# Attention of two layers rebuilt as one staggered stage each, sink heads first, and the scan's convolution done in place

## The chip, the cores and the metric

One core of a Trainium2 chip runs the whole program. The metric is device microseconds of that core, the median of several runs. TensorE (PE; its weight loads are PEld in the profile), VectorE (DVE) and ScalarE (ACT) compute. The weights come through SyncE's DMA queue. GpSimd does nothing.

## The reference, cut to what matters

Two blocks of two layers each act on 256 latent and 256 context tokens of width 1024, everything in float32. Block one has a gated linear attention layer and a state-space layer (SSD), whose scan starts with a depthwise convolution of width 5 and a SiLU. Block two has an even and an odd attention layer, and the odd one ends in a mixture of experts. Of the two attention layers the reference computes:

```python
# even: 8 heads of width 64, rms norm on q and k; latent queries see 256 latent keys with a position bias,
# masked by column, and 256 context keys; context queries see the context keys alone
s_loc = einsum(q, k) * 64**-0.5 + where(col_ok, rpb[...], -1e30)
p = softmax([s_loc, q @ k_ctx.T * 64**-0.5]);  out = p @ [v, v_ctx]
# odd: 8 "c" heads (2 key heads, window of 128, a sink in the denominator), 4 "d" heads, q and k with rms norm and rope
p_c = softmax([window scores, context scores], extra=sink)
p_d = softmax(q1 @ k1.T) - lam * softmax(q2 @ k2.T);  out_d = rms_norm(p_d @ v) * subln_g * (1 - LAM_INIT)
# SSD
xbc = silu(dwconv(xbc, conv_w, conv_b))
```

## The kernel before

Activations are kept transposed (features on partitions, tokens along the free axis). `run` walks a list of stages. Each stage has three streams of instructions, one for TensorE, one for ScalarE and one for VectorE, written out by hand. Within a stage the engines meet only at semaphores. Between two stages stands a barrier (each engine drains and waits for the other two), unless the stage is `joined`. TensorE's products go round six PSUM banks in the order of the stage. `Banks.empty` makes TensorE wait until a bank has been read, `Banks.full` makes a reader wait for its product, and `release` drains and frees. Weights are 2 MB blocks in four slots, which SyncE fills again when `W.used` says that a block is finished.

Even layer, stage by stage: `EvenProject` (24 product tiles: gate b, c, u, then q, k, v; L1587), `BiasLoad` (L1637: ScalarE issues 16 DMAs for the position bias, and TensorE flips the landed rows in six products), `HeadNorm` (L1666: for each of eight head tiles Square on ScalarE, a block-ones product on TensorE, Ln and Exp on ScalarE, a scaling on VectorE), and `Attention` with 32 items of 128 queries (L1719). An item is: score product(s) "s", 0.125 and bias on VectorE into SBUF, maximum and its negative there (L1796 to L1803), exponential with its sum on ScalarE (L1770), reciprocal and normalising on VectorE (L1818, L1822), four or two transposes "t" on TensorE (L1746), a copy on ScalarE (L1780), output products "o" with v as the stationary operand (L1753), and a copy on VectorE (L1809). The scores of item n+1 are issued ahead of the transposes of item n.

Odd layer: `OddProject` (21 tiles, L1926), `HeadNorm` over 13 head tiles with a second pass of 13 rotation products (L1685) for rope, `KeysAndLambda` (L1979: both key heads are doubled over the partitions, and lambda), `Attention` with 16 window items that have a sink, a barrier, `Attention` with 8 differential items of two score maps each (L1825, L1826 combine them), and `SubNorm` (L2009).

The scan, `SsdGroups` (L1312): eight groups of eight steps. While group g steps, group g+1 is projected, convolved on VectorE (L1473, L1475: five taps from `s_raw` into one of two accumulators `s_acc`), put through SiLU on ScalarE (L1440: from `s_acc` into its place, one tile behind each convolution), and transposed. The steps themselves need Exp on ScalarE (L1455, L1459) for steps 4 to 7 of a group. SiLU and Exp are in different table sets of ScalarE.

Of the kernel before, what the change touches and what calls it, by code (L numbers as in the profile page):

```python
# [15 lines left out]
ALU = mybir.AluOpType  # L16
# [3 lines left out]
P = 128  # L20
# [156 lines left out]
def build(nc, I, out, stop=None):  # L177
    ctx = ExitStack()
    with ctx:
# [37 lines left out]
        for n in ("loads", "setup_rows", "sil", "mod_lat", "mod_ready", "centred", "squares", "rstd_used", "root", "normed",  # L217
# [4 lines left out]
                  "free_a", "free_b", "free_c", "free_d", "bias_loads", "rope_in", "convd", "ada_rows", "ada_cols", "ada_copied", "ada_free", "moe_loads", "da_done", "ready", "lam", "picked", "placed", "gate_cols", "overflow_known", "moe_rl", "guest_rows", "guest_copied", "guest_cols", "guest_read"):  # L222
# [1004 lines left out]
        s_acc = arena_at(11168, 2, TOK)  # L1227
# [84 lines left out]
        class SsdGroups(Stage):  # L1312
# [5 lines left out]
            def __init__(self):  # L1318
                N, order = 8 * NG, []

                def ahead(g, n):
# [104 lines left out]
            def act(self, act, B, ch):  # L1426
                for ev in self.order:
# [9 lines left out]
                    if kind == "convolve":  # L1437
                        T = LAT if j == 3 else TOK
                        act.wait_ge(*S("convd").taken("act"))
                        act.activation(self.feat(k, j)[:, 0:T], s_acc[:, j % 2, 0:T], ACT.Silu,  # L1440
                                       bias=vc("conv_b", self.tile(k, j))).then_inc(*S("feat").given())
# [20 lines left out]
            def dve(self, dve, B, ch):  # L1462
                for ev in self.order:
                    kind, k, j = ev
                    i = self.index.get(ev)
                    if kind == "convolve":
# [17 lines left out]
                    if kind == "overlap":  # L1484
                        dve.wait_ge(*S("feat").taken("dve", 2))
# [90 lines left out]
        m_q = arena_at(4096, 8, TOK)  # L1576
# [3 lines left out]
        m_bias = arena_at(13824, 8, 6, GRID)  # L1580
        m_pad = arena_at(15872, 4, 2 * (LAT + 2))
        m_gc = arena_at(6144, 4, TOK)
        m_s = [[uT[:, 2 * i + j, :] for j in range(2)] for i in range(2)]
        m_pt = [uT[:, 4 + i, :] for i in range(2)]
        sinks = sb("sinks", [P, 8])

        class EvenProject(Stage):  # L1587
            products = 24
            joined = True

            def pe(self, pe, B):
                w_in = I["ev_w_in_2"][0]
                for c in range(6):
                    w = W.block(pe, [w_in[:, c * 512:c * 512 + 512]], KD)
                    if c == 0:
                        first_features(pe, B, [(j, w, j * P, P) for j in range(4)], TOK)
                    for j in range(4 if c else 0):
                        if c == 5:
                            token_major(pe, B, 4 * c + j, w, 0, 512, uT, KD, j)
                        else:  # L1600
                            feature_major(pe, B, 4 * c + j, w, j * P, uT, KD, 0, TOK)
                    W.used(full_sem, B.base + 4 * c + 4)

            def act(self, act, B, ch):
                for i in range(8):
                    bank = B.full(act, i)
                    act.activation((m_g if i < 4 else m_gc)[:, i % 4, :], bank[:, :], ACT.Copy).then_inc(*B.free(i))
                for i in range(12, 24, 2):
                    bank = B.full(act, i)
                    act.activation(self.dst(i), bank[:, :], ACT.Copy).then_inc(*B.free(i))  # L1610

            def dst(self, i):
                return [m_q, m_k, m_v][(i - 12) // 4][:, i % 4, 0:512]

            def dve(self, dve, B, ch):
                dve_link(ch, dve.memset(arena[:, 15872:15872 + 8 * (LAT + 2)], 0.0))
                for j in range(4):
# [16 lines left out]

        m_braw = arena_at(16896, 8, 6, GRID)

        class BiasLoad(Stage):  # L1637

# [800 lines left out]
```

## Time and profile before

| | |
|---|---|
| median of three runs | 3602.71 us (3601.45 to 3604.27) |
| time of the profiled execution, its span | 3605.16 us, 3603.4 us |
| TensorE busy, mean granted clock | 3213.0 us (89%), 0.92 |
| VectorE, ScalarE busy | 1328.3 us (37%), 557.3 us (15%) |

| stretch, us from the span's start | what runs |
|---|---|
| 1043 to 1465 | `SsdGroups` |
| 1788 to 1955 | `EvenProject` |
| 1955 to 1999 | `BiasLoad`, `HeadNorm` |
| 1999 to 2140 | `Attention`, even |
| 2683 to 2783 | `OddProject` |
| 2783 to 2828 | `HeadNorm`, `KeysAndLambda` |
| 2828 to 2927 | `Attention`, window items |
| 2927 to 2990 | `Attention`, differential items |
| 2990 to 2997 | `SubNorm` |

A float32 product shows as two MATMUL records, a transpose as one. The granted clock is 1.00 at 2.4 GHz and 0.50 at 1.2 GHz; a value between is a mean over a stretch.

### The profile page before, as it was taken

How to read it: one execution, taken by the hardware profiler on the slowest of the kernel's cores; microseconds unless marked ns; L12 is line 12 of the kernel's file. 1: busy time of each engine (PE TensorE's matmuls, PEld its weight loads, DVE VectorE, ACT ScalarE, POOL GpSimd, SP SyncE). 2: the span in 40 equal slices, each digit the busy share in tenths (PEclk: the TensorE clock that was granted, in tenths of full speed). 3: DMA queues.
4: the chain of work that ended last, by engine and by line, in shares of the span. 5: the costliest groups of instructions: out<-in, count | busy, mean ns of one | idle time of the engine just before them, and what ended most of it. 6: DMA issues, size and time to landing. Idle time of an engine off the chain costs nothing.

```text
span 3603.4 us, 31613 instructions
## 1 busy us (share of the span) xinstructions
PE 3213.0 (89%) x12574; PEld 2029.4 (56%) x12574; DVE 1328.3 (37%) x3165; ACT 557.3 (15%) x1077; POOL 0.2 (0%) x4
## 2 busy tenths in 40 slices
PE   7996889999987877899997779999999666999999
PEld 2446344444565555688743344444455335799998
DVE  2655365477426566411210433533010553001011
ACT  1111110000214334120100321000011222100000
POOL 0000000000000000000000000000000000000000
PEclk9998889999988988899998779999999657999999
DMA  7530145565241111145313002543322002478885
GB/s 247 181 128 1 46 152 187 152 188 189 70 117 47 38 33 47 61 151 150 117 70 87 1 1 94 187 136 105 96 85 91 0 0 71 169 252 289 278 269 204
DMA packets 382833, 431.46 MB, mean 120 GB/s; under 512 B 15257, under 2 KB 291384, under 8 KB 382554
## 3 DMA queue, kind: packets, MB, share of 16 engines
q1 hardware_dynamic: 281840, 329.77, 27.9%
q10 hardware_dynamic: 100842, 99.62, 8.6%
q8 instruction: 102, 1.67, 0.2%
q14 instruction: 49, 0.40, 0.0%
HBM read 428.32 MB, written 1.05 MB: 119 GB/s over the span
## 4 chain that ended last, share of the span: by engine, by line
PE 80%; DVE 11%; ACT 3%; issue 3%; DVEq 1%; DMA 1%; ACTq 0%
PE bank L813 48%; PE bank L2178 9%; PE bank L830 5%; PE bank L2192 4%; PE bank L838 4%; PE bank L1753 2%; PE bank L517 2%; PE bank L1746 1%; DVE arena L1475 1%; DVE small L1800 1%; PE bank L2160 1%; DVE uT L1798 1%; ACT L1455 1%; PE bank L2204 1%; DVE arena L1505 1%
## 5 line engine op out<-in xcount | busy, mean ns | idle before, releaser
L813 PE MATMUL bank<-uT,slot 128*128 128x512 f32 (+2 forms) x2848 | 1071.6, 535 | 2.1 <-DVEq L2364 2.1
L813 PEld LDWEIGHTS bank<-uT,slot 128*128 128x128 f32 (+1 forms) x2848 | 539.2, 191 | 480.9 <-issue 455.4
L813 PE MATMUL bank<-arena,slot 128*128 128x512 f32 (+1 forms) x2016 | 695.7, 507 | 30.6 <-DVEq L2364 30.6
L813 PEld LDWEIGHTS bank<-arena,slot 128*128 128x128 f32 x2016 | 387.7, 194 | 318.8 <-issue 279.0
L560 DVE SCALAR_TENSOR_TENSOR arena<-arena,sT 128x256 f32<-128x256 f32 x784 | 333.7, 481 | 8.0
L2178 PE MATMUL bank<-arena,slot 128*128 128x128 f32 x2816 | 317.6, 276 | 5.1 <-issue 4.4
L2178 PEld LDWEIGHTS bank<-arena,slot 128*128 128x128 f32 x2816 | 316.7, 193 | 7.9 <-issue 7.8
L886 DVE SCALAR_TENSOR_TENSOR hT<-bank,mod,hT 128x256 f32<-128x256 f32 (+1 forms) x104 | 41.6, 439 | 419.2 <-PE bank L813 419.2
L830 PE MATMUL bank<-uT,slot 128*128 128x512 f32 (+1 forms) x448 | 168.5, 541 | 24.4 <-ACT uT L582 12.5
L2263 DVE TENSOR_TENSOR arena<-bank,halves 128x256 f32<-128x256 f32 (+1 forms) x48 | 19.3, 403 | 435.6 <-ACT halves L2224 435.6
L2192 PE MATMUL bank<-slot,arena 128*128 128x256 f32 x704 | 153.3, 379 | 1.0 <-DVEq L144 1.0
L830 PEld LDWEIGHTS bank<-uT,slot 128*128 128x128 f32 x448 | 92.7, 209 | 99.8 <-issue 92.8
L2192 PEld LDWEIGHTS bank<-slot,arena 128*128 128x128 f32 x704 | 133.7, 190 | 19.3 <-issue 1.2
L838 PE MATMUL bank<-slot,uT 128*128 128x512 f32 (+3 forms) x416 | 133.5, 478 | 5.7 <-issue 5.7
L1746 PE MATMUL bank<-const,uT 128*128 128x128 f32 x192 | 50.3, 403 | 94.2 <-DVE uT L1822 63.0
L669 ACT ACTIVATE halves<-hT 128x512 f32<-128x512 f32 (+1 forms) x49 | 26.4, 540 | 576.6 <-DVE hT L886 576.6
L1746 PEld LDWEIGHTS bank<-const,uT 128*128 128x128 f32 x192 | 30.7, 198 | 148.3 <-DVE uT L1822 108.9
L953 DVE TENSOR_TENSOR arena<-halves 128x512 f32<-128x512 f32 (+1 forms) x64 | 35.8, 559 | 202.3 <-ACT halves L943 202.1
L838 PEld LDWEIGHTS bank<-slot,uT 128*128 128x128 f32 x416 | 69.6, 201 | 68.3 <-issue 68.2
L560 DVE SCALAR_TENSOR_TENSOR rstd<-arena,sT,rstd 128x256 f32<-128x256 f32 x224 | 90.0, 480 | 0.0
L1475 DVE SCALAR_TENSOR_TENSOR arena<-arena,vectors 128x512 f32<-128x512 f32 (+1 forms) x128 | 87.7, 685 | 4.6
L517 PEld LDWEIGHTS bank<-const,arena 128*128 128x128 f32 x448 | 61.6, 195 | 41.5 <-issue 27.0
(295 smaller groups left out, 2458.1 us busy)
## 6 DMA issues: line engine op xcount, KB each, us to landing
arena<-in_ada_w ACTq DMA_DIRECT2D x88, 1024.0 KB, 5.2
slot<-in_ffn_w SPq DMA_DIRECT2D x42, 2048.0 KB, 8.9
slot<-in_moe_w SPq DMA_DIRECT2D x32, 2048.0 KB, 10.4
slot<-in_moe_w SPq DMA_DIRECT2D x32, 1408.0 KB, 8.8
slot<-in_moe_w SPq DMA_DIRECT2D x16, 1536.0 KB, 9.2
slot<-in_gla_w_in SPq DMA_DIRECT2D x6, 2048.0 KB, 10.3
slot<-in_ev_w_in SPq DMA_DIRECT2D x6, 2048.0 KB, 8.0
slot<-in_ffn_w SPq DMA_DIRECT2D x8, 1408.0 KB, 6.8
```

Source lines behind the costliest of these rows:

```text
L517: ins = pe.matmul(ada_cols_bank[:, o:o + 1], acc[:, s, j * P:j * P + P], one[:, 0:1], start=True, stop=True)
L560: ins = dve.scalar_tensor_tensor(out=acc[:, s, :], in0=w[:, k, :], scalar=c, in1=acc[:, s, :], op0=ALU.mult, op1=ALU.add)
L813: ins = pe.matmul(bank[0:m, 0:t1 - t0], w[:, k, c0:c0 + m], x[:, k, t0:t1], start=(k == 0), stop=(k == kt - 1))
L830: ins = pe.matmul(bank[0:m, 0:T], w[:, k, c0:c0 + m], uT[:, k, 0:T], start=(k == 0), stop=(k == KD - 1))
L838: ins = pe.matmul(bank[:, 0:c1 - c0], x[:, k, t * P:t * P + P], w[:, k, c0:c1], start=(k == 0), stop=(k == kt - 1))
L886: return dve.scalar_tensor_tensor(out=h, in0=y, scalar=self.m[:, 8 * self.q + k, s:s + 1], in1=h, op0=ALU.mult, op1=ALU.add)
L1455: act.activation(s_cx[k % 2], bank[:, :].rearrange("p (h t) -> p h t", h=4), ACT.Exp).then_inc(*S("ecx").given())
L1475: ins = dve.scalar_tensor_tensor(out=acc, in0=s_raw[:, j, 0:n, tap:tap + LAT], scalar=vc("conv_w", 32 * tap + f), in1=acc, op0=ALU.mult, o ...
L1746: ins = pe.transpose(bank[:, t * P:t * P + P], m_s[n % 2][0][:, t * P:t * P + P], ident)
L1753: ins = pe.matmul(bank[r0:r0 + m, 0:P], v, m_pt[n % 2][:, t * P:t * P + P], start=(t == 0), stop=(t == len(it["v"]) - 1))
L2178: ins = pe.matmul(bank[:, o:o + P], w[:, k, (f - c) * P:(f - c) * P + P], m_x[:, k, e * P:e * P + P], start=(k == 0), stop=(k == KD - 1))
L2192: ins = pe.matmul(bank[:, 0:256], hid[:, k, :], w[:, k, :], start=(k == 0), stop=(k == NFE - 1))
```

## The change

`HeadNorm`, `BiasLoad`, `KeysAndLambda` and `SubNorm` are gone as stages. Their instructions are placed inside the projections and the attention:

- `EvenProject` now runs in the order q, k, b, c, u, v. ScalarE issues the 16 bias DMAs at its start. Eight sums of squares stand between the k and b tiles, seven flips (the bias lies in three pieces) between the c tiles. The bias is kept times 8.
- `OddProject` has 13 sums, 13 rotations ("turn"), the two key doublings ("twin") and lambda between its tiles. VectorE alone takes the q and k tiles out of PSUM; ScalarE takes v.
- There is one `Attention` stage in each layer. The bias is added on TensorE, by a product of the identity and the bias ahead of the latent scores. VectorE takes the maximum from PSUM, and ScalarE's exponential reads PSUM with scale 0.125. Rows are not normalised ahead of the transposes; the output is scaled instead, query by query. In the output product the transposed probabilities are stationary and v moves (64 columns a head, 128 in a differential one), so outputs come with tokens on partitions and are turned back by transposes "f" (four after every 8 even items, two after every 4 window or 2 differential items).
- In the even layer scores run two items ahead, in the odd layer one. The 16 window items come first and the 8 differential ones directly behind them. The norm of a differential output is Square with its sum, Ln and Exp on ScalarE.
- In the scan the convolution accumulates in the tile's final place, and all four SiLUs of a group come behind its last convolution.

```diff
@@ SsdGroups
+                    if n == 4:
+                        out += [("silu", g, j) for j in range(4)]
...
-                        if j >= 2:
-                            dve.wait_ge(*S("feat").taken("dve"))
-                        acc = s_acc[:, j % 2, 0:n * LAT].rearrange("p (s t) -> p s t", s=n)
+                        acc = self.feat(k, j)[:, 0:n * LAT].rearrange("p (s t) -> p s t", s=n)
@@ EvenProject
+                order = [("q", j) for j in range(4)]
+                for j in range(4):
+                    order += [("k", j), ("sum", j)]
+                for j in range(4):
+                    order += [("b", j), ("sum", 4 + j)]
+                for j in range(4):
+                    order += [("c", j), ("flip", 2 * j), ("flip", 2 * j + 1)]
+                order += [("u", j) for j in range(4)] + [("v", j) for j in range(4)]
...
+        def head_sum(pe, B, i, n, T):
+            pe.wait_ge(*S("squares").taken("pe"))
+            bank = B.empty(pe, i)
+            pe.matmul(bank[:, 0:T], half, rl[n % 2][:, 0:T], start=True, stop=True).then_inc(full_sem, 1)
@@ Attention
+                for n in range(-ahead, N + 2):
+                    if n + ahead < N:
+                        order += [("s", n + ahead, j) for j in range(len(items[n + ahead]["maps"]))]
+                    if 0 <= n < N:
+                        order += [("t", n, 0)]
+                    if 0 <= n - 1 < N:
+                        order += [("o", n - 1, 0)]
+                    if n - 2 in turns:
+                        order += [("f", n - 2, 0)]
...
+                            pe.matmul(bank[:, 0:LAT], ident, it["bias"], start=True, stop=False)
+                            pe.matmul(bank[:, 0:LAT], q, k[:, 0:LAT], start=False, stop=True)
+                            pe.matmul(bank[:, LAT:nk], q, k[:, LAT:nk], start=True, stop=True).then_inc(full_sem, 1)
...
-                            ins = pe.matmul(bank[r0:r0 + m, 0:P], v, m_pt[n % 2][:, t * P:t * P + P], start=(t == 0),
+                            ins = pe.matmul(bank[:, 0:w], m_pt[n % 2][:, t * P:t * P + P], v, start=(t == 0),
...
# ScalarE, one turn of the loop over n
+                        act.activation(m_pt[n % 2][:, 0:nk], bank[:, 0:nk], ACT.Copy).then_inc(*B.free(i))
+                            if it["sink"] is not None:
+                                act.activation(es, sinks[:, it["sink"]:it["sink"] + 1], ACT.Exp, bias=nm)
+                            act.activation(s, B[i][:, 0:it["nk"]], ACT.Exp, scale=0.125, bias=nm,
+                                           accum_out=den).then_inc(*B.free(i))
+                            act.drain().then_inc(*S("pr").given())
+                    if 0 <= n - 1 < N and self.items[n - 1]["sub"]:
+                        act.activation(m_turned[:, 0:P], bank[:, 0:P], ACT.Square, accum_out=ssq)
+                        ch.wait(ch(act.drain()))
+                        ch.wait(ch(act.activation(f, ssq, ACT.Ln, scale=1.0 / P, bias=eps)))
+                        act.activation(f, f, ACT.Exp, scale=-0.5).then_inc(*S("root").given())
# VectorE
+                            dve_link(ch, dve.tensor_reduce(mx, bank[:, 0:it["nk"]], AX.X, ALU.max))
...
+                            dve.scalar_tensor_tensor(out=eps, in0=den, scalar=RMS_EPS, in1=den, op0=ALU.mult, op1=ALU.mult)
+                            dve_link(ch, dve.reciprocal(rc1, den1))
+                            dve_link(ch, dve.tensor_scalar(rc, den, rc1, lam_t, ALU.mult, ALU.mult))
+                            dve.scalar_tensor_tensor(out=s0, in0=s1, scalar=rc, in1=s0, op0=ALU.mult,
+                                                     op1=ALU.add).then_inc(*S("pn").given())
...
+                        dve.tensor_scalar(it["o"], bank[:, 0:w], rc, None, ALU.mult).then_inc(*B.free(i))
@@ stages
-        stages += [EvenProject(), BiasLoad(),
-                   HeadNorm(...), Attention(even_items()),
+        stages += [EvenProject(), Attention(*even_attention(), 2),
...
-        stages += [OddProject(), HeadNorm(...), KeysAndLambda(), Attention(window_items()), Attention(diff_items(), lam_t), SubNorm(),
+        stages += [OddProject(), Attention(*odd_attention(), 1),
```

## Rows read from the trace of the kernel before

**Rows 1.** The page: shares of the chain that ended last, TensorE's granted clock in slices.
```profile
PE 80%; DVE 11%; ACT 3%; issue 3%; DVEq 1%; DMA 1%; ACTq 0%
...
PEclk9998889999988988899998779999999657999999
```
**Rows 2.** Busy time by stretches: length, PE, PEld, DVE, ACT, POOL, clock, DMA.
```profile
1203.60:1230.10 26.50, 16.30 (x112) 13.11 (x111) 21.88 (x52) 13.36 (x20) 0.00 (x0) 0.74 0.27 80
...
1788.20:1954.60 166.40, 166.36 (x384) 73.45 (x384) 25.42 (x40) 12.58 (x21) 0.00 (x0) 0.99 0.18 63
1954.60:1998.70 44.10, 16.81 (x29) 5.63 (x28) 10.86 (x15) 14.12 (x24) 0.00 (x0) 0.77 0.36 83
1982.50:1998.70 16.20, 8.71 (x16) 2.46 (x16) 6.01 (x8) 14.00 (x24) 0.00 (x0) 1.00 0.00 0
1998.70:2139.70 141.00, 101.52 (x353) 58.39 (x353) 64.94 (x208) 38.41 (x96) 0.00 (x0) 0.66 0.00 1
...
2683.40:2783.40 100.00, 99.44 (x336) 60.61 (x336) 11.87 (x24) 9.18 (x18) 0.00 (x0) 0.97 0.20 69
2783.40:2828.20 44.80, 24.77 (x58) 10.81 (x58) 25.93 (x58) 17.91 (x41) 0.00 (x0) 0.78 0.14 47
2828.20:2926.60 98.40, 73.76 (x225) 42.88 (x225) 43.43 (x144) 25.58 (x64) 0.00 (x0) 0.55 0.00 1
2926.60:2990.30 63.70, 32.50 (x128) 21.63 (x128) 37.49 (x88) 17.84 (x40) 0.00 (x0) 0.67 0.00 0
2990.30:2996.75 6.45, 1.97 (x9) 1.47 (x9) 2.38 (x6) 4.68 (x12) 0.00 (x0) 0.94 0.00 1
```
**Rows 3.** ScalarE in the scan: table loads, by line and form.
```profile
L1440 ACT ACT_TABLE_LOAD x21 | 26.9, 1283 | 0.4
L1455 ACT ACT_TABLE_LOAD x21 | 26.9, 1283 | 0.4
```
**Rows 4.** The scan, 1092 to 1465: one wait of TensorE; ScalarE in order of time.
```profile
PE bank L1406 <- ACT arena L1451: 41.6, 15, 5.0
...
1209.10 0.72 ACT L1440 ACTIVATE arena<-arena,vectors 128x512 f32<-128x512 f32 x1 [3.44 <-DVE arena L1475]
```
**Rows 5.** Even attention, TensorE in order of time, at the lower clock level.
```profile
2010.54 2.07 PE L1741 MATMUL bank<-arena 64*128 64x512 f32 x2
2013.16 1.97 PE L1753 MATMUL bank<-uT,arena 128*64 128x128 f32 x8
...
2022.02 1.12 PE L1746 MATMUL bank<-const,uT 128*128 128x128 f32 x4 [1.50 <-DVE uT L1822]
2023.07 1.12 PE L1753 MATMUL bank<-uT,arena 128*64 128x128 f32 x4
```
**Rows 6.** The same at the upper level.
```profile
2049.18 1.09 PE L1753 MATMUL bank<-uT,arena 128*64 128x128 f32 x8
2050.20 1.12 PE L1741 MATMUL bank<-arena 64*128 64x512 f32 x2
...
2053.14 0.65 PE L1753 MATMUL bank<-uT,arena 128*64 128x128 f32 x4
2053.72 1.09 PE L1741 MATMUL bank<-arena 64*128 64x256 f32 x2
```
**Rows 7.** Rotation products of the odd `HeadNorm`, six without a wait between them.
```profile
2800.83 2.75 PE L1685 MATMUL bank<-arena,const 128*128 128x256 f32 x12
```
**Rows 8.** Odd attention, 2828 to 2997, by line: ScalarE and VectorE.
```profile
L1770 ACT ACTIVATE uT<-uT,small 128x512 f32<-128x512 f32 x32 | 22.9, 715 | 30.3 <-DVE small L1803 30.3
L1780 ACT ACTIVATE uT<-bank 128x512 f32<-128x512 f32 x24 | 14.3, 598 | 35.2 <-PE bank L1746 35.2
L1770 ACT ACTIVATION_READ_ACCUMULATOR uT<-uT,small 128x1 f32 x32 | 6.0, 188 | 0.0
...
L1800 DVE TENSOR_REDUCE small<-uT 128x1 f32<-128x512 f32 x32 | 22.0, 686 | 4.4
L1826 DVE SCALAR_TENSOR_TENSOR uT<-uT,small 128x512 f32<-128x512 f32 x8 | 6.0, 752 | 0.3
```

More of the change, by code:

```diff
@@ L7 @@
 from contextlib import ExitStack
+import itertools
 import math
@@ L1604, in act @@
[L1604 to L1613, printed above, removed]
@@ new lines, in act @@
+                for n in range(2):
+                    head_square(act, self.head(n)[0], n, TOK)
+                for i, (kind, j) in enumerate(self.order):
+                    if kind == "sum":
+                        rstd_act(act, B, ch, j, i, TOK, 64, RMS_EPS)
+                        if j + 2 < 8:
+                            head_square(act, self.head(j + 2)[0], j + 2, TOK)
+                    if kind in "bc":
+                        bank = B.full(act, i)
+                        act.activation((m_g if kind == "b" else m_gc)[:, j, :], bank[:, :], ACT.Copy).then_inc(*B.free(i))
+                    if kind == "v" and j % 2:
+                        bank = B.full(act, i)
+                        act.activation(m_v[:, j, 0:512], bank[:, :], ACT.Copy).then_inc(*B.free(i))
@@ new lines, in build, with __init__ @@
+        LAM_INIT = 0.8 - 0.6 * math.exp(-0.3)
+        lam_t = small[:, 60:61]
+        sub_gain = small[:, 61:62]
+        class Attention(Stage):
+            def __init__(self, items, turns, ahead):
+                self.items, self.turns, self.ahead = items, turns, ahead
+                self.maps = list(itertools.accumulate(len(it["maps"]) for it in items))
+                N, order = len(items), []
+                for n in range(-ahead, N + 2):
[7 more added lines that the diff above has]
+                        order += [("f", n - 2, 0)]
@@ L1732, in __init__, with score, stats @@
                 self.order = {key: i for i, key in enumerate(order)}
                 self.products = len(order)
+            def score(self, n, j):
+                return m_s[n % 2][j][:, 0:self.items[n]["nk"]]
+            def stats(self, n, j):
+                o = 12 * (n % 4) + 6 * j
+                return [small[:, o + x:o + x + 1] for x in range(6)]
             def pe(self, pe, B):
@@ L1748, in pe @@
                     else:
[L1749 removed]
+                        dst, src, gain, made = self.turns[n]
+                        for m in made:
+                            B.freed(pe, self.order["o", m, 0])
                         bank = B.empty(pe, i)
[L1751 to L1754 removed]
+                        for t, x in enumerate(src):
+                            ins = pe.transpose(bank[:, t * P:t * P + P], x, ident)
@@ L1776, in act @@
+                for n in range(-self.ahead, N + 1):
+                    if 0 <= n < N:
                         i, nk = self.order["t", n, 0], self.items[n]["nk"]
@@ L1839, in even_items, with even_attention @@
+        def even_attention():
+            rows = m_o.rearrange("p (t c) -> p t c", t=4)
+            items, turns = [], {}
             for h in range(8):
@@ new lines, in head @@
+            def head(self, n):
+                kind, j = self.heads[n]
+                x = {"cq": m_ql[:, j, :], "dq": m_ql[:, 4 + j, :], "ck": m_k[:, 0, :], "dk": m_k[:, 2 + j, :]}[kind]
+                return x, f"od_{kind}_g_2", x.shape[1]
+            def pe(self, pe, B):
+                first = dict(cq=0, dq=512, ck=1024, dk=1280, dv=1792)
+                for kind, j in self.order:
+                    i = self.index.get((kind, j))
+                    if kind in first and j == 0:
+                        c = first[kind]
+                        w = W.block(pe, [I["od_w_in_2"][0][:, c:c + (256 if kind == "ck" else 512)]], KD)
+                    if kind == "cq":
+                        if j == 0:
+                            first_features(pe, B, [(n, w, n * P, P) for n in range(4)], LAT)
+                    elif kind == "dq":
+                        feature_major(pe, B, i, w, j * P, uT, KD, 0, LAT)
+                    elif kind == "ck":
```

589 lines of the change are left out of this document (289 added, 300 removed).

## The prediction

> **What bounds the kernel now.** The chain of waits comes first: TensorE carries 80% of it, VectorE 11%, ScalarE 3% [rows 1]. The slices of granted clock beside it show where TensorE is also slow: it is near full almost everywhere, and sags to 0.5 to 0.7 near 2000 us and near 2900 us [rows 1]. Those are the two attention layers. The busy time by stretches then shows three kinds [rows 2]. In the projections TensorE is busy for 166.36 of 166.40 us and 99.44 of 100.00 us at clock 0.97 to 0.99: nothing can be won there but work. Between projection and attention lie 44.1 us (even) and 44.8 us (odd) with 16.8 and 24.8 us of TensorE work, and 6.45 us follow the differential items. In attention itself no engine is full: 141.0 us with TensorE 101.5 at clock 0.66, 98.4 us with 73.8 at 0.55, 63.7 us with 32.5 at 0.67. There the stage is a round trip over three engines, and the clock, which falls in it, stretches TensorE's share of the trip. In the scan a stretch of 26.5 us in each group has TensorE at 16.3 and VectorE at 21.9 [rows 2], and TensorE waits 41.6 us in all for ScalarE's copy L1451, which stands behind an exponential [rows 4].
>
> **The scan.** ScalarE loads a table 42 times in seven groups, 6 a group at 1.28 us [rows 3], because SiLU tiles and exponentials alternate. With the four SiLUs in one place 2 a group are left: 28 loads go, 36 us of ScalarE. More weighs the order: SiLU waits 3.44 us for VectorE's taps [rows 4], and exponentials of the steps queue behind it. What VectorE can give bounds the gain: 26.5 − 21.9 = 4.6 us of idle time in the stretch, and some 2.0 us ahead of it (one load of 1.28 and one SiLU of 0.72), so 6.6 us a group, 46 us. Against it, four SiLUs (three of 0.72, a shorter one) and two loads now make one block of some 5 us, and the exponential of a later step waits behind it; if that block takes all back, the gain is 0. Following the stretch instruction by instruction I get the later steps 4.1 to 4.6 us earlier, so 4.3 x 7 = 30 us.
>
> A switch costs about 2.66 us with its drain by the Trainium skill ("ScalarE: Activation LUTs", What ACT_TABLE_LOAD costs). The load's row of 1.28 us is what the trace has; by the page the 28 switches would be 75 us of ScalarE instead of 36.
>
> **Even layer up to attention.** The 44.1 us go. Into the projections come eight sums of 512 columns and seven flips of 3072 columns together. A record of 512 columns takes 166.4 / 384 = 0.43 us and a product has two [rows 2]: 14 x 0.87 = 12.1 us, with some start cost 13.5. Their feeders are covered: a head costs ScalarE 14.0 / 8 = 1.75 us and VectorE 0.75 us [rows 2], against 6.9 us of TensorE a tile. The bias DMAs are issued first on ScalarE; issue, landing, flips and norm took 44.1 us together, and the first flip comes after 13 tiles, some 90 us. SyncE's queue keeps its order and block sizes. If the cover fails, a sum waits about 2 us. One barrier of some 1.1 us stays.
>
> **Items at the upper clock.** Starts of neighbouring instructions give the price of a group. Output of four blocks: 1.02 us, of two 0.58, scores of 512 columns 1.02 [rows 6], so 0.59 for 256. Four transposes take 1.05 us at the lower level [rows 5], where four output blocks take about 1.9, so 0.57 at the upper one, and two 0.35. The bias product adds 256 columns, 0.43. The new output product loads 128 columns and streams 64 where it loaded 64 and streamed 128; no row shows that. Bounds: half of the old price, and the old one, since the loads would then set the pace. I take the old one, the nearest row. A latent item is 1.45 + 0.57 + 1.02 = 3.05 us of TensorE, a context item 0.59 + 0.35 + 0.58 = 1.52. Two of each and four turning transposes are 9.7 us a head.
>
> The other engines fit under it. ScalarE: copy 0.60, exponential 0.72 + 0.19 [rows 8], some 1.7 us for a latent item. VectorE: maximum 0.69 [rows 8], four small ones of 0.15 to 0.25, some 1.5. The round trip of a window item, where scores run one ahead, is transposes 0.57, copy 0.60, sink exponential 0.30 less overlap, exponential 0.9, handovers: about 2.5 us, under 3.05. So TensorE waits for nobody after the first items: the wait L1746 on L1822 is gone, and late next is TensorE itself. Even attention: 8 x 9.7 = 78, plus 4 for filling and the last turn, 82 us.
>
> Even layer in sum: 44.1 + 141.0 = 185.1 us become 13.5 + 1.1 + 82 = 97: −88.
>
> **Odd layer.** 29 products join the projections: eight sums of 256 and five of 512 columns, 13 rotations, two doublings, lambda. Six rotations took 2.75 us [rows 7], 0.46 each, so 0.6 with a wait before it; 8 x 0.6 + 5 x 1.0 + 13 x 0.6 + 2.3 = 20 us in the place of 44.8. Where a tile is short (1.8 us in "cv") a slot is still 3.0 us, against some 2.2 on VectorE. Window items: 16 x 3.05 and turns, 50.4 us, plus 2.6 barrier and filling, for 98.4. Differential items: TensorE 2.0 + 0.57 + 1.0 = 3.7 us, but the trip is copy 0.6, two exponentials 1.8, combining 0.75 and three small ones 0.6, transposes 0.6, handovers: 4.7 us. TensorE waits 1 us in each and the clock will alternate; at the lower level an item is about 7. I take 5.6: 8 x 5.6 = 45 for 63.7, and 3 us of tail for 6.45. Sum: 44.8 + 98.4 + 63.7 + 6.5 = 213.4 us become 20 + 53 + 45 + 3 = 121: −92.
>
> Together −30 − 88 − 92 = −210 us. The profiled execution took 3605.2 us (span 3603.4), 2.5 above the median of the runs. That gives 3395 against it and 3393 against the median; I forecast 3395.
>
> **Rivals.**
> - *The clock stays at the lower level in attention.* At it a latent item is scores 1.97 + 0.85, transposes 1.05, outputs 1.9, so 5.8 us, a context item 2.8, a head 18.3 [rows 5]: even attention 146 + 5 = 151 us, window items 16 x 6 = 96, differential ones 52. Total −30 − 19 − 41 = −90: 3515. For it: the clock was 0.66 and 0.55 there [rows 2], and a TensorE that is merely denser at half speed may never rise again. Against it: `HeadNorm` kept 1.00 with TensorE busy 8.7 of 16.2 us [rows 2], the new stages enter from projections at full clock with 1.1 us between, and attention then leaves no wait. The Trainium skill gives it a mechanism ("TensorE: Matmul & The Clock Gate", Part 4: PE-mode transpose): transposes don't count as busy for the clock. Transposes are 0.57 of 3.05 us here; by that rule the forecast's busy share is 81% instead of full, and this rival's time could follow.
> - *One of the three attention stages falls and stays low, the others don't:* 3395 + 46 to 69, about 3450. The first barrier and the filling are where it would happen.
> - *The scan gains nothing,* since ScalarE's block stands in the path: 3425. Against: VectorE's idle time [rows 2].
> - *Slower: the interposed products break the projections.* 44 products now stand in TensorE's order behind results of ScalarE or VectorE, and everything behind them waits too. If those waits pull the clock down where 266 us run at full clock [rows 2], the projections cost 266 us more and the total is 3605 − 210 + 266 = 3661. It decides from a share of 210 / 266 = 79% of them at the lower level, or from 4.8 us of wait at each of the 44. Against: 1.75 and 0.75 us of work per head under tiles of 3.4 to 6.9 us.
>
> **How the numbers follow.** Forecast 0.60, one stage low 0.20, all low 0.13, scan nothing (else as forecast) 0.03, slower 0.03, rest 0.01 near no change. The forecast's own band is 3365 (scan at its bound, cheaper output products by some 15 us) to 3425. The range reaches to the one-stage cases and a little on: 3365 to 3500. About 0.2% is what a measurement can tell from no change; faster 0.96, same 0.01, slower 0.03.
>
> **What would show it.** Scan: 16 table loads or so instead of 42, a group near 48 us instead of 52.7. Projections: about 180 and 120 us, TensorE over 95% busy, clock near 1. Attention: even about 82 us, window about 53, clock above 0.9 in both and TensorE busy nearly throughout; differential items near 5.6 us with waits for the combining instruction. Wrong would be: clock near 0.5 with TensorE busy (first rival), waits at the sums (last rival), or output products at half their price.

## The result, and the profile after

| | before | after |
|---|---|---|
| median of the runs | 3603.49 us (4) | 3373.07 us (4; 3371.0 to 3379.0) |
| ratio after/before | | 0.9364, 95% interval 0.9347 to 0.9380 |
| profiled execution, its span | 3605.16, 3603.4 | 3373.84, 3372.1 |
| mean granted clock of TensorE | 0.919 | 0.957 |

The change saves 230 us; 210 were forecast (3395). Where the 231.3 us between the two spans come from is read from where the same stretches begin and end in both traces:

| stretch | before | after | difference | forecast |
|---|---|---|---|---|
| up to the scan's gates (L1267) | 1026.4 | 1021.3 | −5.1 | 0 |
| scan, up to the even projections | 761.8 | 744.8 | −17.0 | −30 |
| even projections and attention | 351.4 | 253.0 | −98.4 | −88 |
| even feed-forward | 543.8 | 542.7 | −1.1 | 0 |
| odd projections and attention | 313.3 | 206.7 | −106.6 | −92 |
| rest | 606.7 | 603.6 | −3.0 | 0 |

The first line is not the change. In the twelve traces of kernels with the new attention (the changed kernel and its variants below) it lies anywhere between 1019.5 and 1027.1, and most of the difference is there at 370 us already, in the first layer, which is the same in all of them. The first, fourth and last line together, 9 us, stand in no term of the forecast. The even layer's difference has some play too: its old attention takes 140.9 us at a mean clock of 0.66 in the trace of before, and 147.7 at 0.56 in that of the scan alone (below), which leaves it as it was.

The page after: TensorE's busy tenths and granted clock in 40 slices, and the chain of waits. The sag near 2000 us and near 2900 us [rows 1] is gone.

```profile
PE   7997789999998788789999999999999988999998
...
PEclk9997889999998889889999999999999988999999
...
PE 86%; DVE 7%; ACT 2%; issue 2%; DVEq 1%; DMA 0%; ACTq 0%
```

Busy time by stretches of the kernel after (columns as in [rows 2]): even projections, odd projections, one group of the scan; then even attention, window items, differential items.

```profile
1766.10:1944.50 178.40, 178.40 (x414) 79.07 (x414) 39.00 (x60) 24.50 (x40) 0.00 (x0) 0.99 0.22 68
2561.80:2677.10 115.30, 115.23 (x394) 71.61 (x394) 37.63 (x87) 26.25 (x54) 0.00 (x0) 0.97 0.17 60
1200.40:1250.30 49.90, 42.03 (x188) 26.96 (x188) 32.76 (x73) 15.70 (x27) 0.00 (x0) 0.89 0.16 48
...
1945.20:2019.10 73.90, 72.02 (x432) 53.58 (x433) 36.79 (x132) 35.47 (x96) 0.00 (x0) 1.00 0.09 29
2677.80:2724.60 46.80, 46.17 (x276) 34.43 (x276) 22.40 (x76) 21.93 (x62) 0.00 (x0) 1.00 0.13 46
2724.60:2768.50 43.90, 30.64 (x160) 20.68 (x159) 27.76 (x84) 25.00 (x76) 0.00 (x0) 0.84 0.00 1
```

In the projections and the first two attention stretches TensorE is busy for 97 to 100% of the time at clock 0.97 to 1.00; VectorE is busy for half of it at most. In the differential items TensorE is busy for 70%, in the scan for 84%. In a differential item the two score products, which lie on different halves of the partitions (64 each), run side by side: they start at 2724.58 and 2724.59, and their four records of 512 columns take 1.13 us, where the two records of one such product alone take 1.12 [rows 6]. The transposes follow 1.06 us behind the start:

```profile
2724.58 1.13 PE L1761 MATMUL bank<-arena 64*128 64x512 f32 x4
2725.64 0.66 PE L1772 MATMUL bank<-const,uT 128*128 128x128 f32 x4
```

One turn of TensorE's items in even attention, in order of time (start, duration, engine, line, operation, count; a stall would stand in brackets). It answers to [rows 6]:

```profile
1987.38 0.61 PE L1788 MATMUL bank<-const,arena 128*128 128x128 f32 x4
1987.83 0.60 PE L1763 MATMUL bank<-arena,const 128*128 128x256 f32 x2
1988.35 0.70 PE L1764 MATMUL bank<-arena 64*128 64x256 f32 x2
1988.89 0.59 PE L1765 MATMUL bank<-arena 64*128 64x256 f32 x2
1989.41 0.44 PE L1772 MATMUL bank<-const,uT 128*128 128x128 f32 x2
1989.68 1.00 PE L1779 MATMUL bank<-arena,uT 128*128 128x64 f32 x8
1990.53 0.65 PE L1763 MATMUL bank<-arena,const 128*128 128x256 f32 x2
```

From start to start: a turning group 0.45 us, latent scores with the bias 1.58, transposes of two blocks 0.27, output of four blocks 0.85. No bracket: nobody is waited for.

In the scan TensorE's wait for ScalarE's copy (41.6 us in [rows 4]) is down to 8.0, and the table loads are 16. But its wait for VectorE's product behind the decays, 30.3 us before, is 52.5. Waits of TensorE, 1092 to 1460 (what waited, for whom: us, times, longest):

```profile
PE bank L1419 <- DVE arena L1521: 52.5, 23, 5.4
...
PE bank L1408 <- ACT arena L1453: 8.0, 8, 1.5
```

### The profile page after: what moved, and what is told of

The parts are those of the page before. It is cut to its first block, busy times and chain, and to the rows that moved or that the text cites. A ratio compares the mean times of both kernels' runs of the same rounds, so it can differ in the third digit from the quotient of the medians.

```text
span 3372.1 us, 31682 instructions
## 1 busy us (share of the span) xinstructions
PE 3124.2 (93%) x12728; PEld 2004.9 (59%) x12728; DVE 1269.7 (38%) x3022; ACT 517.7 (15%) x1064; POOL 0.2 (0%) x4
## 4 chain that ended last, share of the span: by engine, by line
PE 86%; DVE 7%; ACT 2%; issue 2%; DVEq 1%; DMA 0%; ACTq 0%
PE bank L814 51%; PE bank L2248 9%; PE bank L831 5%; PE bank L2262 4%; PE bank L839 4%; PE bank L518 2%; PE bank L1779 1%; DVE arena L1475 1%; PE bank L1772 1%; PE bank L2230 1%; PE bank L2274 1%; DVE arena L1505 1%; PE bank L1105 1%; PE bank L1764 1%; DVE arena L1521 1%
## 5 line engine op out<-in xcount | busy, mean ns | idle before, releaser
L887 DVE SCALAR_TENSOR_TENSOR hT<-bank,mod,hT 128x256 f32<-128x256 f32 (+1 forms) x104 | 41.6, 439 | 415.6 <-PE bank L814 415.6
L1419 PE MATMUL bank<-arena 128*64 128x128 f32 x256 | 35.6, 358 | 52.6 <-DVE arena L1521 52.5
L1964 DVE TENSOR_TENSOR arena<-bank,halves 128x512 f32<-128x512 f32 x22 | 15.2, 692 | 181.5 <-PE bank L814 159.3
```

The source lines that it names most:

```text
L887: return dve.scalar_tensor_tensor(out=h, in0=y, scalar=self.m[:, 8 * self.q + k, s:s + 1], in1=h, op0=ALU.mult, op1=ALU.add)
L1419: pe.matmul(o, s_xdt[k % 2][:, h, :], s_m[k % 2][:, h, :], start=True, stop=False)
```

## The experiments

The theory: the four parts of the gain are independent; in attention TensorE no longer waits, so the clock stays up; where it still waits (differential items), VectorE's own row of work is what paces it. The rivals: the clock is at risk whatever the waits; the scan's gain is the accumulation in place; the interposed sums are fragile. All ratios are to the kernel before on the same chip; the changed kernel's is 0.9364.

**The scan's part alone**, in the kernel before.

```diff
                     if 1 <= n < 5:
                         out += [("convolve", g, n - 1)]
+                    if n == 4:
+                        out += [("silu", g, j) for j in range(4)]
-                        acc = s_acc[:, j % 2, 0:n * LAT]...
+                        acc = self.feat(k, j)[:, 0:n * LAT]...
```

> The kernel before with only the scan's part of the change (convolution in place, four SiLUs in one place). Theory: the parts are independent and the scan gives what the two traces show up to the even layer, 22 us: 3581 us, with 16 table loads, and TensorE's wait for ScalarE's copy (41.6 us) gone, but its wait for VectorE's product behind the decays grown by some 20. Rival A, my prediction's term: 30 us, 3573. Rival B, the 22 us came from elsewhere: within 0.2% of 3603.

Measured: 3584.17 us, ratio 0.9962 (0.9948 to 0.9976). From the gates to the even projections it takes 744.5 us for the 761.8 of before: −17.3, as in the whole change. TensorE's waits, 1050 to 1460:

```profile
PE bank L1419 <- DVE arena L1521: 55.5, 25, 5.4
...
PE bank L1408 <- ACT arena L1453: 7.8, 8, 1.3
```

So the part is additive and worth 17 us in the traces (15 between the medians on this chip), not 22 and not 30. I had taken the 5 us ahead of the gates for a part of it.

**SiLU behind each convolution again**, in the kernel after, accumulation still in place.

```diff
-                        out += [("convolve", g, n - 1)]
-                    if n == 4:
-                        out += [("silu", g, j) for j in range(4)]
+                        out += [("convolve", g, n - 1), ("silu", g, n - 1)]
```

> The changed kernel with the convolution still in place, but each SiLU directly behind its own convolution again, as before. Theory: the gain of the scan is the order on ScalarE (28 table loads and the exponentials behind a waiting SiLU), so some 20 us come back: 3393. Rival: it is the accumulation in place (VectorE no longer waits for SiLU to free one of two buffers), then the time stays within 5 us of 3373.

Measured: 3393.20 us, ratio 0.9432 (0.9416 to 0.9448). The stretch from the gates to the even projections takes 761.8 us, the same as before to a tenth, and the old pair of waits is back:

```profile
PE bank L1406 <- ACT arena L1451: 41.2, 15, 5.0
PE bank L1417 <- DVE arena L1519: 29.5, 31, 3.1
```

The whole gain is the order on ScalarE. The accumulation in place gives nothing by itself; it makes room for the four tiles that the order needs. How much of the order's gain is the 26 table loads fewer and how much the earlier exponentials was not run apart.

**One differential item behind every two window items**, scores still one ahead.

```diff
-            for d, t in itertools.product(range(4), range(2)):
-                diff[d, t] = len(items)
+                d, t = h // 2, h % 2        # inside the loop over the window heads
+                diff[d, t] = len(items)
```

> The changed kernel, but in the odd layer one differential item comes behind every two window items. Theory: the 8 differential items take 41 to 44 us only because three engines wait for each other in turn; TensorE's own work in one is 3.5 us (two scores 2.04, transposes 0.5, outputs 1.0), 28 us for eight. Between window items 3.05 us of other work cover a trip of some 4.1 us, so about 1 us of wait is left in each, and the clock stays up: 7 to 9 us less, about 3365. Rival: VectorE's work is what bounds a differential item, and interleaved it delays the window items too: within 3 us of 3373, or slower.

Measured: 3384.37 us, ratio 0.9405 (0.9390 to 0.9421): slower than the changed kernel. From the first score to the output projection it is 100.0 us for 90.7. TensorE, two differential items (the transposes that wait are theirs) and what follows the second:

```profile
2692.81 0.66 PE L1772 MATMUL bank<-const,uT 128*128 128x128 f32 x4 [1.26 <-DVE uT L1843]
...
2703.43 0.66 PE L1772 MATMUL bank<-const,uT 128*128 128x128 f32 x4 [2.07 <-DVE uT L1843]
...
2705.42 1.22 PE L1764 MATMUL bank<-arena 64*128 64x256 f32 x2
```

The cover (what TensorE does between an item's scores and its transposes) was about right. One ahead, a differential item's transposes come behind transposes, outputs and the next scores: 0.5 + 0.85 + 1.6 = 2.95 us where the neighbours are window items. It is no less than between differential items, where it is 0.5 + 1.0 + 1.06 = 2.6, since two score maps run side by side; the 2.04 us that I had charged for them was wrong. What failed is the trip: it takes 5.0 us from the end of the scores at 2698.39 to the transposes at 2703.43, where I had 4.1. So a wait of 1.2 or 2.1 us, once 3.6, comes in every one of the eight, 14.6 us in all for 11.1 in the changed kernel. Behind the longer ones the clock falls (1.22 us for a part of the scores that takes 0.70 in the changed kernel), which makes TensorE's busy time 82.6 us for 76.8. Why the trip is longer among window items was not taken further.

**The same with scores two ahead.**

```diff
-        stages += [OddProject(), Attention(*odd_attention(), 1),
+        stages += [OddProject(), Attention(*odd_attention(), 2),
```

> As the interleaved one, and scores run two items ahead in the odd layer as in the even one. Theory: the trip of a differential item is now covered by two items, no wait is left, TensorE is full: odd attention 16 x 2.97 + 8 x 3.5 + 2 = 78 us for some 90, so 3361. Rival: VectorE, which takes the maxima of a later item first and then waits for its exponentials, holds up the outputs of earlier ones: no better than with one ahead, about 3366.

Measured: 3358.21 us, ratio 0.9330 (0.9314 to 0.9345). This beats both kernels; the interval lies below that of the changed kernel, 0.9347 to 0.9380. Attention takes 75.6 us for 90.7. Busy time over it:

```profile
2680.80:2755.80 75.00, 71.85 (x432) 52.97 (x432) 49.11 (x160) 46.78 (x136) 0.00 (x0) 0.98 0.08 29
```

**Two ahead, differential heads last.** The same one-word edit in the kernel after.

> The changed kernel (differential heads last) with scores two items ahead in the odd layer. Two things differ between it and the interleaved run that won 15 us: the order of the heads. Theory: behind each other, differential items are bound by VectorE's own row of two maxima, waiting for the exponentials, combining and output (4.6 us an item), whatever the distance; so no gain, within 4 us of 3373. Rival: distance alone removes TensorE's waits and the order doesn't matter: 3360.

Measured: 3367.00 us, ratio 0.9360 (0.9345 to 0.9376), the same as the changed kernel. The odd attention is 86.4 us for 90.7. So distance gives some 4 us, order without distance costs 9, both together give 15. The reason stands in VectorE's row in the kernel after, one turn of differential items:

```profile
2739.76 0.68 DVE L1829 TENSOR_REDUCE small<-bank 128x1 f32<-128x512 f32 x1
...
2741.26 0.15 DVE L1834 TENSOR_SCALAR small<-small 128x1 f32<-128x1 f32 x1
2742.41 0.16 DVE L1840 SCALAR_TENSOR_TENSOR small<-small 128x1 f32<-128x1 f32 x1 [0.99 <-ACTq L1811]
...
2742.99 0.75 DVE L1843 SCALAR_TENSOR_TENSOR uT<-uT,small 128x512 f32<-128x512 f32 x1
2743.66 0.34 DVE L1858 TENSOR_SCALAR arena<-bank,small 128x128 f32<-128x128 f32 x1
2743.92 0.68 DVE L1829 TENSOR_REDUCE small<-bank 128x1 f32<-128x512 f32 x1
```

From maximum to maximum 4.2 us (4.8 in the turns that also copy a turning group), of which VectorE itself waits 1.0 for the exponentials of the item it has just begun. It is a ring of its own, and no distance on TensorE shortens it; between window items, which ask VectorE for some 1.5 us each, its average fits under TensorE's.

**Even attention one ahead.**

```diff
-        stages += [EvenProject(), Attention(*even_attention(), 2),
+        stages += [EvenProject(), Attention(*even_attention(), 1),
```

> The changed kernel with scores only one item ahead in the even layer. Theory: that attention takes 73.9 us because two items of staggering cover the trip over VectorE and ScalarE. One ahead covers a latent item (3.0 us of TensorE), but not a context item (1.4 us for a trip of about 2): half a microsecond to one of wait in 16 items, 8 to 16 us more, 3381 to 3389, and the clock falls only here and there. Rival (the clock): small waits are enough to keep it at the lower level in the whole stage, 60 us more, 3433.

Measured: 3380.35 us, ratio 0.9389 (0.9373 to 0.9404). The stage takes 79.0 us for 73.9. The waits for exponentials are 4.3 us in all, mostly one of 0.43 us a head and not 16, and the clock is 1.00 throughout:

```profile
1965.98 0.66 PE L1772 MATMUL bank<-const,uT 128*128 128x128 f32 x4 [0.43 <-ACTq L1811]
```

The stage loses 5.1 us where 8 to 16 were expected. Waits as short as these (the longest is 0.8 us) didn't touch the clock.

What the other changes inside an item (the bias on TensorE, the exponential from PSUM, the new output product) are worth each was not run.

**Every sum directly behind its head** in the even projections (with ScalarE's squares moved accordingly).

```diff
-                for j in range(4):
-                    order += [("k", j), ("sum", j)]
-                for j in range(4):
-                    order += [("b", j), ("sum", 4 + j)]
+                order += [("sum", j) for j in range(4)]
+                for j in range(4):
+                    order += [("k", j), ("sum", 4 + j)]
+                order += [("b", j) for j in range(4)]
```

> The changed kernel with every head sum of the even projections directly behind its own head, so that each waits for VectorE's copy and ScalarE's square. Theory: a sum then waits about 1.8 us (four of them) or less (the first four follow each other), 8 to 15 us in all, and the clock stays near full in the projections: 3381 to 3388. Rival (the slower case of the prediction): such waits pull the clock down where 180 us run at full speed; half of that stretch at the lower level would be 90 us more, 3463.

Measured: 3389.27 us, ratio 0.9418 (0.9402 to 0.9433). Projections and attention take 262.3 us for 253.0. TensorE:

```profile
1803.66 1.12 PE L1600 MATMUL bank<-halves,const 128*128 128x512 f32 x2 [1.10 <-ACT halves L1594]
...
1806.37 7.03 PE L814 MATMUL bank<-uT,slot 128*128 128x512 f32 x16
1814.85 1.13 PE L1600 MATMUL bank<-halves,const 128*128 128x512 f32 x2 [1.45 <-ACT halves L1594]
```

Four waits of 1.45, one each of 1.10 and 0.63: 7.5 us of the 9.3, and a tile behind a wait still takes 7.03 us. The clock of the projections stays at 0.99. The mechanism of my slower rival costs little but its waits; it would have needed 4.8 us a wait.

**A pause ahead of each attention.** All engines wait while ScalarE makes a chain of copies.

```diff
+        class Pause(Stage):
+            def act(self, act, B, ch):
+                for _ in range(self.n):
+                    ch.wait(ch(act.activation(uT[:, 0, :], uT[:, 0, :], ACT.Copy)))
...
+        stages += [EvenProject(), Pause(8), Attention(*even_attention(), 2),
+        stages += [OddProject(), Pause(40), Attention(*odd_attention(), 1),
```

> The changed kernel with a pause of all engines but ScalarE (a chain of copies of one row) ahead of each attention: 8 copies, about 6 us, ahead of the even one, 40 copies, about 30 us, ahead of the odd one. Theory: what kept the clock low in the old attention was its own waits, not how it was entered, so each pause costs its length, and the dense attention behind it gets the clock back within a few items: 40 to 48 us more, 3413 to 3421. Rival (the clock stays at the lower level once TensorE has been idle): 62 us more in the even layer or 45 to 75 more in the odd one, each beside the pauses: 3470 or above.

Measured: 3497.67 us, ratio 0.9722 (0.9706 to 0.9738): +124.6 us, of which only 32 are the pauses (6.16 and 27.30 us of idle time for 0.72 each). My theory fell. TensorE's first groups in even attention and, 13 us ahead of the end of the stage, scores behind a turning group:

```profile
1949.93 1.22 PE L1773 MATMUL bank<-arena,const 128*128 128x256 f32 x2 [6.16 <-ACTq L2437]
1951.09 1.22 PE L1774 MATMUL bank<-arena 64*128 64x256 f32 x2
...
2061.58 0.72 PE L1773 MATMUL bank<-arena,const 128*128 128x256 f32 x2
2062.23 0.70 PE L1774 MATMUL bank<-arena 64*128 64x256 f32 x2
```

For 112 us nobody is waited for, TensorE is busy the whole time, and the granted clock is 0.50; then it rises in the middle of the same pattern. The odd one is the same for 81 us. The stage takes 125.2 us for 73.9, and 128.0 for 90.7. Two stretches of the kernel with pauses:

```profile
1949.90:2010.00 60.10, 60.07 (x187) 42.40 (x187) 16.36 (x58) 15.29 (x44) 0.00 (x0) 0.50 0.02 6
...
2761.90:2800.00 38.10, 38.10 (x114) 26.65 (x114) 9.32 (x30) 9.65 (x27) 0.00 (x0) 0.50 0.00 1
```

**A shorter pause:** 3 copies ahead of the even attention, 8 ahead of the odd one.

> As the kernel with pauses, with 3 copies (some 2 us) ahead of the even attention and 8 (6 us) ahead of the odd one. In the run before, 6 us ahead of the even attention left TensorE at the lower level for 112 us though it then waited for nothing. Theory: it is the length of the idle time that decides, and somewhere between the 0.7 us of a plain barrier and 6 us lies the point; 2 us is short of it, 6 us ahead of the odd attention is beyond it: 9 us of pauses and some 40 in the odd layer, 3422. Rival: every idle time beyond a barrier does it: 60 us more in the even layer too, 3482. Second rival: the even case was a matter of place, and neither falls: 3382.

Measured: 3426.73 us, ratio 0.9506 (0.9490 to 0.9522). TensorE, the first group of each stage:

```profile
1948.83 0.70 PE L1773 MATMUL bank<-arena,const 128*128 128x256 f32 x2 [2.85 <-ACTq L2437]
...
2688.20 1.22 PE L1773 MATMUL bank<-const 128*128 128x256 f32 x2 [6.15 <-ACTq L2437]
...
2774.90 2.08 PE L1771 MATMUL bank<-arena 64*128 64x512 f32 x4
...
2787.46 1.08 PE L1789 MATMUL bank<-arena,uT 128*128 128x128 f32 x8
```

After 2.85 us of idle time the stage takes 73.9 us, at 1.00 throughout; after 6.15 the odd one stays at 0.50 for 99 us and takes 132.3. Here the rise, at 2787, comes 12 us after the first scores of differential items, so the work had changed before it. As both places fell after some 6 us, it isn't a matter of the place. What lies between 2.85 and 6.15 us was not run.

**Transposes at full clock:** 400 between the even projections and attention, which nothing reads.

```diff
+                for i in range(self.n):
+                    ins = pe.transpose(bank[:, 0:P], uT[:, i % KD, 0:P], ident)
```

> The changed kernel with 400 more transposes of 128 by 128, back to back, between the even projections and the even attention; nothing reads them. A transpose is 0.12 us at full clock in the attention items (four in 0.49 us), so 49 us more, 3422, if the clock stays where it is, as it did in attention where transposes are a sixth of the work. Rival (transposes do not count as busy for the clock): the clock falls within the stretch, the rest of the 400 take twice as long and attention behind it starts at the lower level: 60 to 100 us more, 3433 to 3473.

Measured: 3417.51 us, ratio 0.9491 (0.9471 to 0.9511), +44.4.

```profile
1944.22 43.88 PE L1732 MATMUL bank<-const,uT 128*128 128x128 f32 x400 [0.72 <-ACTq L2443]
```

```profile
1949.00:1970.00 21.00, 21.00 (x195) 21.00 (x193) 0.00 (x0) 0.00 (x0) 0.00 (x0) 1.00 0.08 30
```

The clock stays at 1.00 through 44 us of nothing but transposes, and attention behind them runs at it too. The rule of the Trainium skill that the prediction weighed ("TensorE: Matmul & The Clock Gate", Part 4: PE-mode transpose) isn't what this chip does with these transposes.

**Work between pause and attention:** 8 copies of pause in both layers, then 24 products of 512 columns in the even one, 192 transposes in the odd one.

> The changed kernel with 8 copies of pause (6 us) ahead of each attention, and between pause and attention work that nothing reads: 24 products of 512 columns (10.4 us at the upper level, 20.8 at the lower) in the even layer, 192 transposes (21 us, or 42) in the odd one. Theory: what does not bring the clock back is the mixture of short operations in attention, not the pause; dense products of 512 columns do, as in the output projections behind attention, so the even attention runs at full speed again: 6 + about 16 us more there instead of 56. Whether transposes do is what the odd place tells: if they count like products, 6 + some 30 us and full speed behind them; if they don't count for the clock, 42 us at the lower level, and attention behind them stays low (45 us more), about 95 in all. Sum: 3431 with transposes counting, 3490 with not. Rival: nothing but time brings the clock back: both attentions stay low for 60 to 110 us from the pause.

Measured: 3432.68 us, ratio 0.9520 (0.9504 to 0.9536). By stretches, the products, then the attention behind them; the transposes, then the window items:

```profile
1952.20:1955.00 2.80, 2.75 (x4) 1.21 (x5) 0.00 (x0) 0.00 (x0) 0.00 (x0) 0.50 0.35 122
1955.00:1958.00 3.00, 3.00 (x5) 1.32 (x4) 0.00 (x0) 0.00 (x0) 0.00 (x0) 0.50 0.00 0
1958.00:1961.00 3.00, 3.00 (x8) 1.21 (x7) 0.00 (x0) 0.00 (x0) 0.00 (x0) 0.95 0.00 0
1961.00:1976.00 15.00, 15.00 (x36) 6.39 (x34) 0.00 (x0) 0.00 (x0) 0.00 (x0) 1.00 0.00 0
1976.40:2049.40 73.00, 72.11 (x432) 53.59 (x432) 36.11 (x131) 35.47 (x96) 0.00 (x0) 1.00 0.00 1
2715.70:2718.00 2.30, 2.23 (x11) 2.24 (x12) 0.00 (x0) 0.00 (x0) 0.00 (x0) 0.50 0.49 178
2718.00:2721.00 3.00, 3.00 (x22) 3.00 (x21) 0.00 (x0) 0.00 (x0) 0.00 (x0) 0.75 0.00 0
2721.00:2738.00 17.00, 17.00 (x158) 17.00 (x157) 0.00 (x0) 0.00 (x0) 0.00 (x0) 1.00 0.01 2
2739.00:2786.00 47.00, 46.29 (x276) 34.59 (x278) 22.39 (x76) 22.08 (x62) 0.00 (x0) 1.00 0.00 1
```

Both kinds bring the clock back within the first few microseconds, and both attentions then take their full-speed time (73.9 and 89.6 us). Transposes do it as well as wide products. The total agrees with the first branch of the theory, but partly by luck: a product of 512 columns is two records of 0.43 us, so 24 are 20.8 us at the upper level; I had charged half, and had allowed too long a stretch at the lower level.

**Projections and convolutions of the scan a step earlier**, on top of the best version.

```diff
-                    out = [("project", g, n)] if n < 4 else []
-                    if 1 <= n < 5:
-                        out += [("convolve", g, n - 1)]
+                    out = [("project", g, j) for j in {0: (0, 1), 1: (2,), 2: (3,)}.get(n, ())]
+                    if n < 4:
+                        out += [("convolve", g, n)]
```

> The interleaved kernel with two ahead in the odd layer, and in the scan the next group's first two projections in one step and every convolution one step earlier. Theory: in the steps 4 to 7 of a group VectorE is what TensorE waits for (4.7 us at once behind the third convolution, 7 us a group), and that convolution now lies beside a projection: 2 to 4 us less a group, 14 to 28 us less in all, 3330 to 3344. Rival: TensorE also loses the projection that stood beside the first of these steps, and waits as much as before: within 5 us of 3358.

Measured: 3373.79 us, ratio 0.9364 (0.9345 to 0.9383), where the version that it builds on has 0.9330: by the ratios 12 us slower (15.6 between the medians, which come from two chips), worse than either theory. The scan's stretch accounts for 10.6 of them, 755.1 us for 744.5. A group takes 52.0 us (mean of six periods between SiLU's table loads) for 50.1, and TensorE waits for VectorE's product 31 times, where it was 55.4 us in 25:

```profile
PE bank L1419 <- DVE arena L1521: 59.2, 31, 4.3
```

The projection was cover for the step in which VectorE has a convolution and the decays; without it the wait comes in that step. That is the rival's mechanism, read from the order and not tested apart; why it costs more than it gives was not taken further.

## Why the prediction was right, and where it was off

The forecast was 3395, the result 3373. The parts miss by more than the sum: 25 us too little for the two attention layers, 13 too much for the scan, and 9 in stretches that the change doesn't touch. That the first two partly cancel is luck.

- **The clock and the round trip: right.** "Attention then leaves no wait": the clock is 1.00 in 121 us of even and window attention. Of my arguments against the first rival the one that carried is the entry "from projections at full clock with 1.1 us between" (it is 0.72); that no wait is left was not needed, since scores one ahead leave waits of up to 0.8 us at clock 1.00. How long a gap the entry bears I did not know: 2.85 us were borne, 6.15 were not. At the lower level for all but its last 13 us the new even stage takes 125.2 us, against the old one's 141.0, so 51 of its 67 us of gain hang on the entry. The pauses show that rival at work in its own words, a TensorE that is denser at half speed and does not rise, for 81 to 112 us. Its price for a head at the lower level (18.3 us) was 10% high; the turning groups there are 33.2 us apart, for two heads.
- **Even layer: −98.4 for −88.** Projections +12.0 (13.5 forecast) and a barrier of 0.72 (1.1). Attention 73.9 (82): two heads take 17.83 us from turning group to turning group where I had 2 x 9.7. I charged four turning transposes of 0.57 to each head; they come once in two heads and take 0.45, so 0.35 us a head. Output products take 0.85 and 0.49 us, not the old price of 1.02 and 0.58 [rows 6]: 0.5 us a head. The old price was an upper bound.
- **Odd layer: −106.6 for −92.** The products in the projections +15.9 with the barrier (20 and a barrier), the window items 46.8 (53), differential items with their tail 43.9 (48). Their period is 4.5 us, where I had 5.6 by weighing in more of the lower clock; it alternates as foreseen, 0.84 in the mean. TensorE's own part was too high: the sum 2.0 + 0.57 + 1.0 is 3.6, not 3.7, and the two score products take 1.06 us together, not 2.0, so it is 2.6 and the wait 1.4 in the mean (11.1 us in eight). The trip forecast, 4.7 us, was close to the period, but it's VectorE's ring that sets it.
- **The scan: −17.0 for −30, the one term too high.** "VectorE's idle time bounds the gain" held as a bound, but the step "the later steps come 4.1 to 4.6 us earlier" failed. A group takes 50.2 us in the mean for 52.7. ScalarE's wait left TensorE's path, and VectorE's was standing right behind it: of the 33.6 us that TensorE no longer waits for the copy, 22.2 come back as a longer wait for the product behind the decays (30.3 to 52.5 us), since VectorE has the third and fourth convolution ahead of them. That leaves 11 of the 17 us. In the whole stretch TensorE is idle for 12 us less; the other 5 us are its own busy time, 646.0 us for 651.2 with the same work, at a slightly higher clock (0.88 for 0.87 while groups run). With the scan's part alone the same 17 us are 8 and 9. The prediction quotes 2.66 us for a switch; the traces bear out 1.28: in that of before a load of 1.28 us starts at 1209.84 and the exponential at 1211.13, and ScalarE's busy time falls by 33.3 us for 26 loads.
- **The slower rival:** its mechanism costs 9 us where provoked, with the clock at 0.99.

## What to carry to other kernels

Before a removed wait is priced, follow what is second latest at the same place; here the runner-up took back two thirds of the scan's wait. In a staggered stage count the cover of one item as what its engine does until it needs the result, with the neighbours that the order really gives it and their rows from start to start, and check that no engine's own loop, waits inside it included, is longer: order and distance only paid together. A dense stage of short operations should be entered from dense work; a few microseconds of idle time ahead of it can cost it half its speed for a hundred.

## What the hardware showed that was not expected

- TensorE, busy all the time in attention's mixture (64-row scores, transposes, outputs of 64 columns), stayed at the lower of its two levels (1.2 GHz) for 112, 81 and 99 us after idle times of 6.16, 27.30 and 6.15 us. Then it rose, in the first two cases without a change in the work, in the third 12 us after differential items had begun. Pure streams of transposes or of 512-column products rose within about 6 us from the same idle time. The same mixture entered at the upper level (2.4 GHz) stayed there, even with waits of 0.4 to 0.8 us (4.3 us in all), and after 2.85 us of idle time. Which part of the mixture keeps it low was not isolated.
- An output product with 128 columns stationary and 64 moving takes 0.85 us for four blocks, one with 64 stationary and 128 moving 1.02 [rows 6]: 17% less, though it loads twice the columns.
- Two float32 products of 64 rows and 512 columns, one from partitions 0 to 63 and one from 64 to 127, start within 0.01 us of each other and take 1.13 us together, where one alone takes 1.12 [rows 6].
- 400 transposes run at 0.110 us each, one after another, at the clock 1.00.
- At some 360 us, ahead of everything that the variants change, twelve traces lie up to 6 us apart (360.7 to 366.6 for the same product, L1105), and the old even attention took 140.9 and 147.7 us in two; a difference of a few us between two profiles is looked for by stretches before it is explained.
